# S5 scan: VectorE turns step q+1's drive between step q's sums and step q's scans

## The reference, cut to what matters

```
lam_bar = jnp.exp(lam * dt)
b_bar   = ((lam_bar - 1.0) / lam)[..., None] * lax.complex(b_re, b_im)
bu      = lax.complex(einsum('bsgp,gnp->bsgn', u, b_bar.real),
                      einsum('bsgp,gnp->bsgn', u, b_bar.imag))
# combine: (a1, x1), (a2, x2) -> (a1 * a2, a2 * x1 + x2)
_, hs   = lax.associative_scan(combine, (a, bu), axis=1, reverse=reverse)
y       = einsum('gpn,bsgn->bsgp', c, hs).real        # y_fwd + y_bwd + d_skip * h
```

## Time and profile before

| what | value |
|---|---|
| time, median of 3 runs | 3180.91 us (3179.99 to 3181.38) |
| profiled execution: its time | 3185.31 us |
| profiled execution: its span | 3183.2 us |
| mean granted TensorE clock over the span | 0.901 |
| PE busy over the span | 2717.1 us (85%) |
| DVE busy over the span | 1709.8 us (54%) |
| S5 steps: first phase to last y_out | 322.02 us to 565.11 us |

### The profile page before, as it was taken

The page is one execution under the profiler, slowest core; times in us unless marked ns, Lnnn a source line. Parts: engine busy times, 40 slices in busy tenths (PEclk is TensorE's granted clock), DMA queues, the critical chain, the costliest instruction groups (busy, mean ns, idle before and its releaser), DMA issues. The chain is left out here.

```text
span 3183.2 us, 48991 instructions
## 1 busy us (share of the span) xinstructions
PE 2717.1 (85%) x18790; PEld 2471.6 (78%) x18796; DVE 1709.8 (54%) x2589; ACT 1258.5 (40%) x2071; POOL 568.4 (18%) x443
## 2 busy tenths in 40 slices
PE   6995788899699978999899856879978888888897
PEld 6995344799589767899799845679978777778797
DVE  3556999455465444455455574345555733334554
ACT  2443555444354323344244452234434722223343
POOL 1001566100076100000000030000037222221000
PEclk9998899999799978999899976689988988888999
DMA  4454000345243531355155331035524300003352
GB/s 158 145 172 147 1 1 1 106 159 194 88 154 132 172 66 21 133 180 176 53 180 186 132 105 68 26 106 187 179 97 162 106 1 1 1 1 105 109 183 92
DMA packets 101124, 340.84 MB, mean 107 GB/s; under 512 B 15888, under 2 KB 20528, under 8 KB 100336
## 3 DMA queue, kind: packets, MB, share of 16 engines
q1 hardware_dynamic: 100976, 338.85, 32.1%
HBM read 337.71 MB, written 1.10 MB: 106 GB/s over the span
## 5 line engine op out<-in xcount | busy, mean ns | idle before, releaser
L134 PE MATMUL ps<-h_high,hi 128*128 128x256 f32 x2936 | 847.9, 289 | 30.2 <-DVE h_low L190 16.7
L111 DVE TENSOR_TENSOR lo<-raw,hi 128x1024 fp32r<-128x1024 f32 x537 | 654.1, 1231 | 386.5 <-ACT hi L101 386.0
L101 ACT ACTIVATE hi<-raw 128x1024 fp32r<-128x1024 f32 x623 | 650.0, 1055 | 514.6 <-PE ps L136 514.6
L135 PE MATMUL ps<-h_low,hi 128*128 128x256 f32 x2936 | 836.7, 285 | 0.0
L136 PE MATMUL ps<-h_high,lo 128*128 128x256 f32 x2936 | 836.1, 285 | 0.0
L134 PEld LDWEIGHTS ps<-h_high,hi 128*128 128x128 f32 x2936 | 569.0, 194 | 47.8 <-DVE h_low L190 20.4
L135 PEld LDWEIGHTS ps<-h_low,hi 128*128 128x128 f32 x2936 | 569.5, 194 | 1.8 <-issue 1.7
L136 PEld LDWEIGHTS ps<-h_high,lo 128*128 128x128 f32 x2936 | 569.4, 194 | 0.0
L135 PE MATMUL ps<-hidden_l,hi 128*128 128x256 f32 x1056 | 298.8, 283 | 0.0
L136 PE MATMUL ps<-hidden_h,lo 128*128 128x256 f32 x1056 | 298.3, 282 | 0.0
L134 PE MATMUL ps<-hidden_h,hi 128*128 128x256 f32 x1056 | 296.1, 280 | 0.0
(11 more groups left out here) (399 smaller groups left out, 4578.2 us busy)
## 6 DMA issues: line engine op xcount, KB each, us to landing
raw<-in_weights SPq DMA_DIRECT2D x623, 512.0 KB, 3.3
at_bias<-bias_group SPq DMA_DIRECT2D x64, 64.0 KB, 2.7
consts<-in_consts SPq DMA_DIRECT2D x1, 1794.5 KB, 9.2
x<-in_x SPq DMA_DIRECT2D x1, 1024.0 KB, 4.8
s_b_raw<-in_s_b SPq DMA_DIRECT2D x1, 1024.0 KB, 5.2
s_c_raw<-in_s_c SPq DMA_DIRECT2D x1, 1024.0 KB, 7.2
at_bias<-bias_groups SPq DMA_DIRECT2D x16, 64.0 KB, 2.7
out<-x SPq DMA_DIRECT2D x1, 1024.0 KB, 3.9
```

The lines of the kernel that those rows point to most:

```text
L101: act.activation(k.hi[:, item % CUT, :], k.raw[:, item % RAW, :], ACT.Copy).then_inc(k.item_rounded, 1)
L111: engine.tensor_tensor(k.lo[:, item % CUT, :], k.raw[:, item % RAW, :], k.hi[:, item % CUT, :].bitcast(F32), ALU.subtract)\
L134: pe.matmul(out, wh, xh, start=start, stop=False, **more)
L135: pe.matmul(out, wh, xl, start=False, stop=False, **more)
```

## The change

- VectorE's program order. Before: angle(q+1), turn(q), sums(q), scans(q). Now: angle(q+2), sums(q), turn(q+1), scans(q), with angle(0), angle(1) and turn(0) ahead of the first step.
- Banks. Drives that have been turned now have two banks (5 and 6), and `mod` has two buffers. Turns, the plain product of time and angle, have one bank (7) instead of two, so phase(q) waits for angle(q-1) instead of angle(q-2).
- The wait for the scans moves from L751 to the product ahead of it, and asks for the scans of two steps before the turned one.
- TensorE's and GpSimd's programs are as before, also in the order and the counts that they wait for.

```diff
-TURN_BANK = 5
-ANGLE_BANKS = 6, 7
+TURN_BANKS = 5, 6
+ANGLE_BANK = 7
...
-                    if q >= 2:
-                        act.wait_ge(s_ang.s, q - 1)
+                    if q >= 1:
+                        act.wait_ge(s_ang.s, q)
...
-                angle(0)
-                for q, (kt, j, d) in enumerate(order):
-                    c = cidx(kt, j, d)
-                    if q + 1 < ST:
-                        angle(q + 1)
-                    s = q % 2
+                def turned(q):
+                    return k.ps[:, TURN_BANKS[q % 2], :].rearrange("p (a n) -> p a n", a=2)
+                def turn(q):
                     cosb = spread(tab[:, q % 3, 0:1, :], 1, 2)
                     sinb = spread(tab[:, q % 3, 1:2, :], 1, 2)
                     bu = k.ps[:, DRIVE_BANKS[q % 3], :].rearrange("p (a n) -> p a n", a=2)
                     dve.wait_ge(s_bu.s, q + 1)
                     dve.wait_ge(s_tab.s, q + 1)
-                    dve.tensor_tensor(mod[:, :, :], bu, sinb, ALU.mult)
-                    if q:
-                        dve.wait_ge(s_scan.s, q)
-                    dve.tensor_tensor(bm, bu, cosb, ALU.mult).then_inc(s_free.s, 1)
+                    if q >= 2:
+                        dve.wait_ge(s_scan.s, q - 1)
+                    dve.tensor_tensor(mod[:, q % 2, :, :], bu, sinb, ALU.mult)
+                    dve.tensor_tensor(turned(q), bu, cosb, ALU.mult).then_inc(s_free.s, 1)
+                angle(0)
+                angle(1)
+                turn(0)
+                for q, (kt, j, d) in enumerate(order):
+                    c = cidx(kt, j, d)
+                    s = q % 2
+                    bm = turned(q)
+                    if q + 2 < ST:
+                        angle(q + 2)
                     dve.wait_ge(s_free.s, q + 1)
-                    dve.tensor_tensor(bm[:, 0, :], bm[:, 0, :], mod[:, 1, :], ALU.add)
-                    dve.tensor_tensor(bm[:, 1, :], bm[:, 1, :], mod[:, 0, :], ALU.subtract).then_inc(s_bm.s, 1)
+                    dve.tensor_tensor(bm[:, 0, :], bm[:, 0, :], mod[:, s, 1, :], ALU.add)
+                    dve.tensor_tensor(bm[:, 1, :], bm[:, 1, :], mod[:, s, 0, :], ALU.subtract).then_inc(s_bm.s, 1)
+                    if q + 1 < ST:
+                        turn(q + 1)
                     dve.wait_ge(s_bm.s, q + 1)
```

More of the change, by code:

```diff
@@ L660, in s5 @@
         with nc.sbuf_tensor([P, 2, T], F32) as ph, nc.sbuf_tensor([P, 2, 3, T], F32) as ang, \
-                nc.sbuf_tensor([P, 3, 2, T], F32) as tab, nc.sbuf_tensor([P, 2, T], F32) as mod, \
+                nc.sbuf_tensor([P, 3, 2, T], F32) as tab, nc.sbuf_tensor([P, 2, 2, T], F32) as mod, \
                 nc.sbuf_tensor([P, 2, 2, T], F32) as g, \
@@ L668, in s5 @@
             tvec = const(k, "time")
-            bm = k.ps[:, TURN_BANK, :].rearrange("p (a n) -> p a n", a=2)
             v1 = V.n
@@ L705, in phase @@
                     c = cidx(*order[q])
-                    if q >= 2:
-                        act.wait_ge(s_ang.s, q - 1)
+                    if q >= 1:
+                        act.wait_ge(s_ang.s, q)
                     act.activation(ph[:, q % 2, :], tvec, ACT.Identity, scale=y[:, c:c + 1], bias=k.round_c[:, 0:1])
-                    act.activation(k.ps[:, ANGLE_BANKS[q % 2], 0:T], tvec, ACT.Copy, scale=y[:, c:c + 1]).then_inc(s_phase.s, 1)
+                    act.activation(k.ps[:, ANGLE_BANK, 0:T], tvec, ACT.Copy, scale=y[:, c:c + 1]).then_inc(s_phase.s, 1)
                 act.wait_ge(V.s, v1)
@@ L734, in angle @@
                         dve.wait_ge(s_tab.s, q - 1)
-                    dve.scalar_tensor_tensor(ang[:, q % 2, 0, :], ph[:, q % 2, :], -ROUND, k.ps[:, ANGLE_BANKS[q % 2], 0:T],
+                    dve.scalar_tensor_tensor(ang[:, q % 2, 0, :], ph[:, q % 2, :], -ROUND, k.ps[:, ANGLE_BANK, 0:T],
                                              ALU.add, ALU.subtract).then_inc(s_ang.s, 1)
-                angle(0)
-                for q, (kt, j, d) in enumerate(order):
-                    c = cidx(kt, j, d)
-                    if q + 1 < ST:
-                        angle(q + 1)
-                    s = q % 2
+                def turned(q):
+                    return k.ps[:, TURN_BANKS[q % 2], :].rearrange("p (a n) -> p a n", a=2)
+                def turn(q):
                     cosb = spread(tab[:, q % 3, 0:1, :], 1, 2)
```

## The result

The changed kernel takes 3248.69 us (median of 4 runs, 3247.05 to 3250.11) against 3180.89: ratio 1.0213, 95% interval 1.0196 to 1.0231. It is 67.8 us slower. The direction was forecast, the size was not: 3211 us was predicted, with 3203 to 3225 as the range. The profiled execution took 3247.05 us, with a span of 3244.9, which is 61.7 more than the span of before. The S5 steps took 303.7 us (321.5 to 625.2) instead of 243.1, so 60.6 of the 61.7 lie there; the block began 0.6 us earlier, and what follows took 2619.8 us instead of 2618.1. In the median the distance is larger by 6 us, because the profiled execution of before lay 4.4 us over its median and that of after 1.6 us under its own.

The account below looks back on a forecast made before the run. VectorE was taken to set the pace at 3.61 us a step, then a loop over TensorE at 4.06. Terms +1.6, +22.7, +1.6, +0.4 and +4.4 gave +30.7 on 3180.9, said as 3211 us, range 3203 to 3225.

Parts of the forecast that it names:

- 0.31 + 0.34 + 0.34 + 0.60 + 0.60 + 1.18 = 3.37 us a step: VectorE's S5 step: same seven instructions without waiting on the one just before, 0.24 us less than 3.61.
- both unseen starts: VectorE starts not in the trace: product to scans taken at 0.60 (other end 0.72), sum to product 0.34 (0.46).
- The sum is 8.13 us for two steps: Loop scans, GpSimd, y, drive, products, scans: 4.06 us a step against VectorE's 3.37.
- I expect the steps to come in pairs: S5 steps alternate between 3.37 and 4.76 us; in the longer VectorE waits 1.39 us for the drive.
- Tables and angle bank hidden: ScalarE's tables loop takes 3.19 us a step, under 3.37; the angle bank costs nothing in the steady state.
- y_out is hidden: VectorE's y_out, 0.39 us seven times, falls where VectorE is about to wait; before it was on the path.
- first scans at 328.9: Start of the S5 steps: first scans come at 328.9 instead of 327.30 us, +1.6.
- drive 3 is waited for behind it: +1.6: At the start, y(0) at half clock takes 3.51 instead of 1.91 us and delays drive 3, +1.6 us.
- The terms without falls: S5 start, step intervals, half-clock y(0) and end: +1.6, +22.7, +1.6 and +0.4 us, 26.3 in all.
- I take 2.2, and two falls again: +4.4: Clock falls in the S5 steps: each costs 2.2 us (1.0 to 2.7), two as before, +4.4 us.
- Rival B: TensorE's clock falls oftener as it works 72% of the time; six falls, +39.5, 3220 us; chance 0.16.
- at half clock ... TensorE has no gap: At half clock y and drive need 5.43 us a step, over the loop's 5.3; argued against +110 us throughout.

Follow-up runs that it names:

- e_after_drive3: Changed kernel with TensorE one drive further ahead (drive(q+3) instead of drive(q+2) ahead of y(q)): 3166.72 us, ratio 0.9945.
- e_after_drive_long: Changed kernel with the first of the two drive matmuls done twice, so three matmuls per drive: 3262.46 us, ratio 1.0258.
- e_after_fill2: Changed kernel with two extra, unneeded matmuls per step behind drive(q+2), in TensorE's gap: 3214.56 us, ratio 1.0101.
- e_before_mod2: Kernel before with the product of drive and sine done twice, first into a buffer nothing reads: 3221.65 us, ratio 1.0122.
- e_after_fill_front: Changed kernel with one extra, unneeded matmul per step ahead of drive(q+2) instead of behind it: 3244.08 us, ratio 1.0207.

## Why the prediction was wrong in size, step by step

- "0.31 + 0.34 + 0.34 + 0.60 + 0.60 + 1.18 = 3.37 us a step": right. 3.35 in e_after_drive3, where nothing else binds; both unseen starts were at the end that was taken. So on these rows a wait for VectorE's own last write costs 0.12 us. The Trainium skill, VectorE: DVE Perf Modes, section "The DRAIN you can't avoid", states of a run of copies that a semaphore after each costs nothing extra. The sums and products here differ from that: an operation that waits for the one before it starts 0.72 us after a product and 0.46 after a sum, one that does not starts after 0.60 and 0.34, and the measurement decides.
- "The sum is 8.13 us for two steps": right. 8.10 in the changed kernel, 8.11 with two fills; e_after_drive3 takes it away, e_after_drive_long stretches it.
- "I expect the steps to come in pairs", 3.37 and 4.76: wrong at 443 to 452 us, where VectorE waits about 0.6 us in each step; with two extra matmuls the waits alternate between 0.79 and 0.42 us. The sum over two steps is the same. Waits of some 43 us in all were forecast, and without falls they were 38.6 (e_after_fill2, in 51 steps).
- Tables and angle bank hidden: right. VectorE waited for a table once, 0.8 us, as it had before, and the bank alone gave 0.9998. That y_out is hidden was not tested by itself.
- "first scans at 328.9", +1.6: near. They came at 328.56, in an execution whose block began 0.5 us earlier. "drive 3 is waited for behind it: +1.6": too small. The clock stayed at the lower level until 341.6 us instead of 334.5, so the drive and the next output ran at half clock too, and VectorE waited 3.96 and 1.16 us for them.
- The terms without falls came to +26.3; measured with the falls taken out, +28, in part by luck: the start cost more than was forecast, but the first step, counted at 4.06 us, had no wait in it, and the loop ran at 8.10 instead of 8.13 in each pass.
- "I take 2.2, and two falls again: +4.4": this is the step that failed. Not the price: 32.5 us over 19 falls is 1.7 each for a mean length of 5.2 us, where 1.0 to 2.7 was worked out for 6.8. The count failed: 19 instead of two, some 32 us instead of 4.4. Rival B named the mechanism, with TensorE at work 72% of the time, and was given 0.16 and six falls. The prediction's own working had both numbers: that a step would be longer by 0.45 us with the same work of TensorE in it, and that another stage, 80% busy, ran at 0.57 for 40 us. The count of falls was nevertheless carried over from the kernel before as if it did not hang on the step. With the measured cost in its place, 26.3 + 32.5, the sum comes to 3240 us; of the 9 that are left to 3249, 6 are the place of the two profiled executions within their kernels' runs (4.4 over the median, and 1.6 under). With the prediction's own 2.2 for each of 19 falls it would have been 3249, but that is luck: nine of the 19 were only 3.4 us long.
- "at half clock ... TensorE has no gap", so that it comes back: right for what was seen. TensorE was busy all of the fall from 460 to 465 us, and the clock came back each time; then TensorE waited again and the clock fell again.

## What to carry to other kernels

When an instruction is moved a step earlier, follow what feeds it through every in-order engine back to itself and divide by the number of steps that the loop spans: here the reordering shortened VectorE's step by 0.25 us and the loop's span from three steps to two, and the loop won. The cure was on the other engine: with the drive one step further ahead the same change is 0.55% faster than the kernel before instead of 2.1% slower. And when a change makes TensorE wait in a loop that it is itself part of, price the loop at full clock and again with many stretches at half clock; in this case the second part was the larger one.

## What the runs showed of the hardware that was not expected

- The number of falls of the granted clock went with how much of a step TensorE had work for: in the S5 steps none to two falls with 2.91 us of work in 3.61 (three kernels with the order of before), none with 2.91 in 3.35, 19 with 2.91 in 4.05, 15 with 2.91 in 4.21, and 3 and 1 when useless matmuls were put into the wait. One or two useless matmuls per step made the program some 35 us faster. Where between these the change comes, and why the falls are 3.4 us long at one time and 6.8 at another, stays open. The share of work is not the whole of it: in e_after_drive_long one fall lasted 20.5 us, and after it 85 us passed without one, where the same instructions had fallen every 10 us.
- A fall need not cost anything: 99 us at half clock were free in e_before_mod2 and cost 32.5 us in the changed kernel.
- Two matmuls with 32 columns each, on different columns of the array, ran beside each other without being asked to: in e_after_fill_front their records alternate 0.03 us apart (355.77 and 355.80), and the pair added nothing to y's 1.85 us.
